# Rounded matrix products that take their moving columns and write PSUM from the last column to the first, in a one-core transformer kernel

## The reference

```
first part, twice:
    h = h + 0.5 * swiglu_ffn(rms_norm(h), w_in, w_out)          # 1024 -> 2 x 2816 -> 1024
    h = h + hybrid_mixer(rms_norm(h), ...)                      # stick-breaking heads and gated-delta heads
    h = h + memory_cross_attention(rms_norm(h), rms_norm(mem))  # 256 memory rows, 4 heads of 256
    h = h + 0.5 * swiglu_ffn(rms_norm(h), w_in, w_out)
second part, twice:
    h = h + concat(forgetting_attention, dilated_attention) @ w_out
    h = h + (p_i @ w_ple) * sigmoid(rms_norm(h) @ w_ple_gate)
```

## Time and profile before

| | |
|---|---|
| median of 3 runs | 3072.54 us (3072.42 to 3076.57) |
| the profiled execution's own time | 3071.89 us |
| its span, first to last instruction | 3070.1 us |
| granted TensorE clock, mean over the span | 0.999 |
| matmuls | 19178 |
| matmuls of L346 and L3365 | 8790 and 5628 |

### The profile page before, as it was taken

How to read it: one execution, slowest core, us unless ns; L and a number is a source line. 1 busy time by engine, 2 the same in 40 slices (tenths; PEclk the granted TensorE clock), 3 DMA queues, 4 the chain that set the end, 5 groups by cost and what they waited for, 6 DMA issues and landing times.

```text
span 3070.1 us, 45342 instructions
## 1 busy us (share of the span) xinstructions
PE 3037.7 (99%) x19178; PEld 2603.2 (85%) x19178; DVE 1990.5 (65%) x2741; ACT 1498.1 (49%) x2083; POOL 150.3 (5%) x158
## 2 busy tenths in 40 slices
PE   9999999999999999999999999999999999999999
PEld 7999887888789998989887788789998886888777
DVE  7667439855584866758447855576675568554774
ACT  5444436553453544435335653454444558454673
POOL 0000000300000000000000200000000006000150
PEclk9999999999999999999999999999999999999999
DMA  4232321132122322232221122122222220222202
GB/s 158 99 115 99 115 72 66 43 124 83 69 97 90 112 97 102 97 116 96 104 83 69 56 85 109 55 96 97 109 98 101 94 83 29 81 104 83 83 31 88
DMA packets 49545, 275.29 MB, mean 90 GB/s; under 512 B 5312, under 2 KB 8896, under 8 KB 26304
## 3 DMA queue, kind: packets, MB, share of 16 engines
q1 hardware_dynamic: 49344, 272.40, 25.1%
HBM read 270.28 MB, written 2.10 MB: 89 GB/s over the span
## 4 chain that ended last, share of the span: by engine, by line
PE 92%; DVE 5%; ACT 2%; issue 1%; DMA 0%; POOL 0%; DVEq 0%; SPq 0%; ACTq 0%; POOLq 0%
PE banks L346 61%; PE banks L3365 22%; PE banks L2612 1%; PE banks L2653 1%; ACT weights L2993 1%; DVE weights L3041 1%; PE banks L1682 1%; PE banks L1832 1%; PE banks L1648 0%; PE banks L1668 0%; ACT slab_hi L314 0%; DVE weights_turned L3062 0%; PE banks L1845 0%; PE banks L3784 0%; PE banks L1703 0%
## 5 line engine op out<-in xcount | busy, mean ns | idle before, releaser
L314 ACT ACTIVATE slab_hi<-slab_raw 128x2048 fp32r<-128x2048 f32 (+2 forms) x207 | 351.7, 1699 | 638.9 <-PE banks L346 615.0
L346 PE MATMUL banks<-x_hi,slab_hi 128*128 128x512 f32 x1488 | 589.1, 396 | 2.5 <-DVE x_lo L433 2.1
L346 PE MATMUL banks<-x_hi,slab_lo 128*128 128x512 f32 x1488 | 580.2, 390 | 0.0
L346 PE MATMUL banks<-x_lo,slab_hi 128*128 128x512 f32 x1488 | 580.0, 390 | 0.0
L321 DVE TENSOR_TENSOR slab_lo<-slab_raw,slab_hi 128x2048 fp32r<-128x2048 f32 (+2 forms) x203 | 409.6, 2018 | 181.6 <-ACT slab_hi L314 181.4
L3365 PE MATMUL banks<-x_blocks_hi,x_area_parts 128*128 128x256 f32 x1736 | 399.4, 280 | 0.0
L346 PE MATMUL banks<-hidden_parts,slab_hi 128*128 128x512 f32 x1280 | 394.3, 389 | 0.0
L346 PEld LDWEIGHTS banks<-x_hi,slab_hi 128*128 128x128 f32 x1488 | 279.7, 188 | 67.9 <-issue 8.7
L346 PEld LDWEIGHTS banks<-x_lo,slab_hi 128*128 128x128 f32 x1488 | 279.9, 188 | 59.5 <-issue 2.9
L346 PEld LDWEIGHTS banks<-x_hi,slab_lo 128*128 128x128 f32 x1488 | 279.6, 188 | 58.9
L3365 PE MATMUL banks<-x_blocks_hi,slab_lo 128*128 128x256 f32 x1072 | 299.2, 279 | 0.0
(11 more groups left out here) (458 smaller groups left out, 5466.0 us busy)
## 6 DMA issues: line engine op xcount, KB each, us to landing
slab_raw<-slabs SPq DMA_DIRECT2D x195, 1024.0 KB, 4.8
slab_raw<-slabs SPq DMA_DIRECT2D x64, 704.0 KB, 4.0
slab_raw<-slabs SPq DMA_DIRECT2D x16, 640.0 KB, 3.8
h<-xT SPq DMA_DIRECT2D x8, 256.0 KB, 5.8
memory<-memT SPq DMA_DIRECT2D x2, 1024.0 KB, 5.4
out<-h SPq DMA_DIRECT2D x7, 256.0 KB, 4.9
constants<-con SPq DMA_DIRECT2D x1, 1284.5 KB, 9.8
slab_raw<-slabs SPq DMA_DIRECT2D x4, 256.0 KB, 5.2
```

Of the source, the lines that this page charges most:

```text
L314: self.nc.scalar.activation(self.wh[:, g % self.HIGHS, 0:w], self.raw[:, g % self.RAWS, 0:w], ACT.Copy).then_inc(self.hi_ready, 1)
L346: mm = self.nc.tensor.matmul(out, left[a], right[c], start=start and n == 0, stop=stop and n == 2)
```

## The change

Two lines and one helper. `down` gives a view of the same memory with the columns in the opposite order (both free dimensions, where there are two). It is applied to the output and to the moving operand of every rounded product; the stationary operand, the flags, the order of the instructions, the waits and all other matmuls stay.

```
+def down(a):
+    return a[:, ::-1] if len(a.shape) == 2 else a[:, ::-1, ::-1]
...
     def products(self, out, left, right, start, stop):
         for n, (a, c) in enumerate(((0, 0), (0, 1), (1, 0))):
-            mm = self.nc.tensor.matmul(out, left[a], right[c], start=start and n == 0, stop=stop and n == 2)
+            mm = self.nc.tensor.matmul(down(out), left[a], down(right[c]), start=start and n == 0, stop=stop and n == 2)
         return mm
...
             for a, c in ((0, 0), (0, 1), (1, 0)):
-                mm = self.k.nc.tensor.matmul(out, left[a], right[c], start=start and n + a + c == 0,
+                mm = self.k.nc.tensor.matmul(down(out), left[a], down(right[c]), start=start and n + a + c == 0,
                                              stop=n == self.BLOCK - 1 and a == 1, skip_group_check=True)
```

## The result

The changed kernel takes 3129.88 us (median of 4, 3128.96 to 3132.51) against 3072.65 us before: a ratio of 1.0188, 95% interval 1.0176 to 1.0200, slower by 57 us. The forecast was no change, with a range that ended at 3111 us. It was wrong.

A forecast was written before the change was run, and what follows sets the result against it. TensorE's product stream was taken to bound the kernel; with every term of the change at zero the sum stayed at 3071.89 us, and the median was forecast unchanged at 3072.5 us, range 3034 to 3111 us.

The forecast's parts named there:

- What bounds the kernel: TensorE, busy 3037.7 of 3070.1 us at 2.4 GHz; any change to a product's pitch reaches the end almost in full.
- The counts and the parts costed at nothing: 14418 matmuls keep their places; no added instruction, wait or byte; weight loads, slab loads, VectorE and ScalarE work: nothing.
- I take the cheap end, zero: Rounded products' columns: falling addresses cost zero, since wide products with one jump take 227.0 ns, the same as plain ones.
- A few cycles per product (slower): Start of each product, fetching a first line or pair: 3.2 and 2.0 ns each, 38.4 us, 3111 us; chance 0.10.
- Half rate: TensorE's path fetching or storing two neighbouring columns at once: pairs form only on rising addresses, 2252 us more, 5325 us; 0.18.
- The change does nothing: Both views are turned back on the way to the instruction; forecast's time, sharing the 0.64 for no effect.
- The same, with the other sign: Time beside the columns: backward reads may meet other accesses less often, 38.4 us less, 3034 us; chance 0.08.
- no effect: Whole kernel within 0.2%, by a free direction or by views turned back; likeliest range 3066 to 3079 us, chance 0.64.
- the 11 to 13.5 ns beside the columns: Time each rounded product takes beyond one column per cycle, cause unnamed; plain float32 matmuls pay only 2.7 ns.
- my own step size: 3.2 ns per 512-column and 2.0 ns per 256-column product, from spread among same-width forms; sets range ends 3034 and 3111 us.

The follow-up runs named there:

- e2: Changed kernel with only the output written backwards, moving operand read forwards: 3071.45 us, ratio 0.9996.
- e4: Changed kernel with read and write backwards in runs of 128 columns, each run forwards: 3072.88 us, ratio 0.9999.
- e13: Kernel before with falling runs, each forwards: 64 columns in 512-column products, 16 in the 256-column products of L3371 and its kin: 3085.38 us.
- e9: Changed kernel with runs of 4 columns in rising order, each run read and written backwards: 3072.35 us.
- e8: Changed kernel with read and write backwards in runs of 32 columns, each run forwards: 3097.83 us.
- e1: Changed kernel with only the moving operand read backwards, sums written forwards: 3130.79 us, ratio 1.0190.
- e16: Kernel before with only the seven-product scheme's 256-column products in falling runs of 32 columns, all others forwards: 3067.75 us, ratio 0.9984.
- e14: Kernel before with 512-column products in rising runs of 32, each backwards, and 256-column ones in falling runs of 64, each forwards: 3119.29 us.
- e3: Changed kernel with read and write backwards in runs of 4 columns, each run forwards: 3127.57 us, ratio 1.0180.
- e10: Changed kernel with four runs of 128 columns in rising order, each run backwards: 3131.29 us.
- e5: All forwards as before the change, but two of three products of a set use only 64 of 128 stationary columns: 3088.28 us.
- e11: All forwards, every product but the first and last of its group using only 32 of 128 stationary columns: 3081.34 us.

## Why the prediction was wrong

**What bounds the kernel** held. TensorE kept 99% of the span at an unchanged granted clock (0.999 before, 1.000 after), and each nanosecond on the pitch of a product came out at the end almost undiminished.

**The counts and the parts costed at nothing** held: 14418 products, no new wait, no change for the other engines, the write to PSUM free (e2).

**The step that failed** is "I take the cheap end, zero", the term for the read of the moving columns. I drew it from the "wide" products, whose read jumps once in 512 columns, and said that "a column at a time needs only that the next address is known in time, which it is with either sign". The runs show 5.9 to 6.6 ns per 512-column product and 10.8 us / 5628 = 1.9 ns per 256-column one. One jump in 512 columns was no test of 127 falling groups: e4 and e13 show that a few long runs, even in falling order, are free, and the wide products' two long runs are of this kind. The Trainium skill's "SBUF — State Buffer" (the paragraph on 16-byte cachelines) agrees with e9, since the order inside 16 bytes is free, but its condition of a second hit in each line is met by the backward read as well, and that one loses 6.6 ns.

**The rivals.** "A few cycles per product (slower)" had the right sign and two thirds of the size: 3.2 and 2.0 ns where 5.9 and 1.9 were measured, 38.4 us in place of 57. For long products the price was nearly twice mine, because I took it from the spread between forward products, which has nothing to do with direction; for short ones it was right by chance. Its place, the start of each product where a first line or pair is read, is refuted by e8 and e9: with runs of 32 a product begins with 32 rising columns and pays in full, turned inside runs of 4 it begins falling and pays nothing. "Half rate" would have shown some 113 us for 264 products; it is out by far, and with the two halves in turn the stream still keeps 250 ns, not 429.4. "The change does nothing" is out by the result itself, and e1 and e2 tell the two views apart. "The same, with the other sign" was wrong for this change. Cheaper orders do exist for 256 columns, runs of 32 (e8, e16) and in some stretches runs of 64 (e14); that reads meet less often in them is not shown.

**The chances.** I gave 0.64 to no effect and 0.28 to slower. The argument for the first rested on rows that, as the text itself said, only failed to speak against it, and the 11 to 13.5 ns beside the columns stood there as a loss without a cause, four to five times what plain float32 matmuls pay. A stream that already loses something unexplained is not one to call indifferent to a change of that read, and a range that ended with my own step size had no room for a step of another size.

**What stays open** is the mechanism. Shown: the loss is in the moving read (e1, e2). With read and write in the same order, it comes from the order of groups of columns within a product and not from where the product begins (e3, e4, e8 to e10), it does not grow with the number of falling steps, and it is tied to how the stream settles. Not shown: what it settles against. The number of stationary columns takes part, as e5 and e11 move the forward pitch, but the backward 512-column pitch stays at 233.3 ns with a quarter of the weights, so the weight load cannot be the whole of it. The partial orders were never tried on the read or the write alone, so the 250 ns of the two halves in turn and the gain of runs of 32 may lie on either side. The stationary operand read backwards was not tried.

## What to carry to other kernels

Where TensorE streams one 4-byte column per cycle and bounds the kernel, let the moving operand rise through memory; at 512 columns falling runs of 64 and 128 were free, and falling runs of 4, 8 and 32 cost 3% of each product; at 256 columns runs of 4 and 16 cost 2%. The order in which the sums are written may be chosen freely between forwards and backwards. For an edit that touches every product, price the smallest disturbance per product times the count first: here 6 ns times 8010.

## What the runs showed of the hardware that was not expected

The pitch of rounded products takes few values: 226.8 and 233.3 ns for 512 columns in nearly all orders; 113.3, 117.8 and 120.0 ns for 256 (104.72, 108.83 and 110.87 us over 924). With the clock at 2.4 GHz these are 544 and 560 cycles, and 272, 283 and 288: all but the 283 are multiples of 16, to within half a cycle. This is an observation without a cause. The same order can settle at two of the values within one execution, and within one stretch of it. Fewer stationary columns can slow the stream: 59.87 us for 264 products with full weights, 60.53 with half in two of three products, 61.07 with a quarter in nearly all.
